# Differential-attention group of a two-layer encoder: another split of PSUM's eight banks, and most scores issued a step earlier

## The reference

```python
logits = jnp.einsum('bqhid,bshid->bhiqs', qb, k).astype(f32) * scale
bias = -slopes[:, None, None, None] * jnp.abs(qp[:, None] - pos[None, :])[None, None]
p = jax.nn.softmax(logits + bias, axis=-1)
a = (p[:, :, 0] - lam * p[:, :, 1]).astype(v.dtype)
return jnp.einsum('bhqs,bshe->bqhe', a, v)
```

## Time and profile before

| | |
|---|---|
| Runs of the kernel before | 2979.78, 2980.28, 2980.36 us; median 2980.28 |
| Profiled execution | 2979.33 us, of which the span of its instructions is 2977.5 us |
| Group C, first layer | unit 8's first transposes start at 358.83 us, unit 15's at 481.40 us |
| Granted TensorE clock, mean | 0.996 |

### The profile page before, as it was taken

How to read it: one execution, slowest core, us unless ns; L and a number is a source line. 1 busy time by engine, 2 the same in 40 slices (tenths; PEclk the granted TensorE clock), 3 DMA queues, 4 the chain that set the end, 5 groups by cost and what they waited for, 6 DMA issues and landing times.

```text
span 2977.5 us, 36876 instructions
## 1 busy us (share of the span) xinstructions
PE 2894.3 (97%) x13564; PEld 2312.8 (78%) x13564; DVE 1996.1 (67%) x2316; ACT 1320.5 (44%) x1843; POOL 461.6 (16%) x243
## 2 busy tenths in 40 slices
PE   7999889999999999999999998899999999999998
PEld 6777656888888888888877785578888888888887
DVE  3987887992465555556678788889716565565555
ACT  4326888993322212222333287889824222212223
POOL 1211332233300000000131123322342000000002
PEclk9999999999999999999999999999999999999999
DMA  5455332432122111111135643234312111112102
GB/s 196 152 170 127 84 81 63 92 82 88 43 64 64 43 42 56 42 42 42 40 133 197 169 97 71 64 86 92 112 44 71 43 55 45 42 42 57 55 29 57
DMA packets 236372, 236.48 MB, mean 79 GB/s; under 512 B 59488, under 2 KB 199520, under 8 KB 236256
## 3 DMA queue, kind: packets, MB, share of 16 engines
q1 hardware_dynamic: 236256, 234.94, 27.9%
HBM read 184.04 MB, written 50.86 MB: 79 GB/s over the span
## 4 chain that ended last, share of the span: by engine, by line
PE 87%; DVE 6%; issue 4%; ACT 2%; DMA 1%; SPq 0%; POOL 0%; ACTq 0%; DVEq 0%
PE ps L1815 31%; PE ps L1830 16%; PE ps L1554 16%; PE ps L1654 8%; PE ps L1726 6%; PE ps L1692 3%; PE ps L1693 3%; DVE ps L1255 2%; PE ps L1688 2%; PE ps L1795 1%; PE ps L1585 1%; PE ps L1739 1%; DVE prob L1327 1%; DVE r L1240 0%; DVE rinv L1322 0%
## 5 line engine op out<-in xcount | busy, mean ns | idle before, releaser
L1654 PE MATMUL ps<-stack 128*128 128x512 f32 (+1 forms) x1152 | 346.0, 418 | 44.1 <-ACT prob L928 19.1
L1453 DVE TENSOR_TENSOR xT<-ps,xT 128x512 f32<-128x512 f32 x352 | 241.5, 691 | 210.1 <-PE ps L1830 209.8
L1654 PEld LDWEIGHTS ps<-stack 128*128 128x128 f32 (+1 forms) x1152 | 205.9, 190 | 154.6 <-ACT prob L928 51.2
L1726 PEld LDWEIGHTS ps<-cst,prob 128*128 128x128 f32 x2048 | 254.7, 142 | 89.6 <-issue 19.8
L1726 PE MATMUL ps<-cst,prob 128*128 128x128 f32 x2048 | 310.7, 275 | 7.8 <-issue 4.1
L928 ACT ACTIVATE prob<-ps,nmx 128x1024 f32<-128x1024 f32 x256 | 284.7, 1112 | 22.7 <-PE ps L1726 12.3
L1363 DVE TENSOR_TENSOR ptl<-ps,pth 128x512 fp32r<-128x512 f32 x384 | 259.4, 685 | 48.8 <-ACT pth L990 42.2
L1418 DVE SCALAR_TENSOR_TENSOR cv<-u,vec,cv 128x1024 f32<-128x1024 f32 x176 | 225.8, 1283 | 89.0 <-ACT cv L1069 78.7
L1081 ACT ACTIVATE ah<-cv 128x1024 fp32r<-128x1024 f32 x44 | 46.7, 1061 | 528.9 <-DVE cv L1431 528.9
L1815 PE MATMUL ps<-xgh,w0h 128*128 128x512 f32 x704 | 274.7, 390 | 0.0
L1815 PE MATMUL ps<-xgl,w0h 128*128 128x512 f32 x704 | 273.9, 389 | 0.0
(11 more groups left out here) (247 smaller groups left out, 5565.4 us busy)
## 6 DMA issues: line engine op xcount, KB each, us to landing
wraw<-in_w_up SPq DMA_DIRECT2D x88, 512.0 KB, 4.9
draw<-in_w_down SPq DMA_DIRECT2D x22, 1024.0 KB, 4.9
stack<-ka_d SPq DMA_DIRECT2D x64, 256.0 KB, 5.8
wraw<-in_w_in SPq DMA_DIRECT2D x30, 512.0 KB, 4.1
vst<-v_d SPq DMA_DIRECT2D x48, 256.0 KB, 3.8
x_d<-xT SPq DMA_DIRECT2D x2, 4096.0 KB, 17.9
wraw<-in_w_out SPq DMA_DIRECT2D x16, 512.0 KB, 5.5
stack<-qc_d SPq DMA_DIRECT2D x64, 128.0 KB, 3.4
```

The source lines that it names most:

```text
L1453: ins = dve.tensor_tensor(xs, ps[:, 4 + j % 4, :], xs, ALU.add)
L1654: ins = pe.matmul(score_banks(i)[:, kh, :], st[q][0:rows, c0:c0 + P], st[k][0:rows, kh * HALF:(kh + 1) * HALF], start=n == 0, stop=n == le ...
L1726: ins = pe.transpose(ps[:, 4 + s % 2, m * P:(m + 1) * P], prob[:, b, m, s * P:(s + 1) * P], ident)
```

## The change

- For C from its third unit on (unit 10), scores go to three pairs of banks (0-1, 2-3, 4-5) by the table `PAIRS`. Units 8 and 9 keep two pairs.
- All of C has one transposing bank (6) and one value bank (7). The factor goes to bank 2 (bank 5 in units 8 and 15).
- TensorE, for items of units from 10 on: item 0 in step 5, item 1 in 6, item 2 in 7, items 3, 4, 5 in steps 0, 1, 2; items 6 and 7 stay in steps 4 and 5, and step 3 has no score. Items 1 (from unit 11) and 2 to 5 wait for the exponential three items back; items 0, 6 and 7 still wait for that of two items back. For unit 10, items 0 and 1 are both in step 6 (the latter waits for two items back).
- Each step's transposes wait for ScalarE's copy of the step before (`pt_hi`).
- Value product 0 of a unit (step 3) waits until the unit before has been read out of the value bank (`o_ready`, in unit 8 `o_read`).
- The factor's transposes move from step 6 to step 3, after that value product; they wait for the exponential of item 3. ScalarE's copy of the factor moves from step 7 to step 4.
- VectorE's `sum_output` in step 3 moves from behind item 5's maximum to ahead of it. In unit 8 ScalarE's `copy_part` moves ahead of the exponential of step 3.

VectorE's order of maxima and mixes and ScalarE's order of exponentials are otherwise as they were.

```diff
-        def score_banks(i):
-
-            return ps[:, 2 * ((i + 1) % 2):2 * ((i + 1) % 2) + 2, :]
+        PAIRS = (1, 2, 0, 1, 2, 0, 2, 0)
+        NORM_PAIR = 1
+        def score_pair(x, i):
+            c = x["k"] - U_C
+            if x["group"] != "C" or c < 2:
+                return (i + 1) % 2
+            return PAIRS[i]
+        def score_banks(x, i):
+            n = 2 * score_pair(x, i)
+            return ps[:, n:n + 2, :]
+        def trans_bank(x, s):
+            return ps[:, 6 if x["group"] == "C" else 4 + s % 2, :]
+        def value_bank(x):
+            return 7 if x["group"] == "C" else 6 + x["half"]
+        def norm_bank(x):
+            if x["group"] != "C":
+                return 7 - x["half"]
+            return 5 if x["k"] in (U_C, U_A - 1) else 2 * NORM_PAIR
+        def score_steps(x):
+            if x["group"] != "C":
+                return STEP_OF[own_items(x)]
+            return STEP_OF[6] if x["k"] < U_C + 2 else {0: 3, 1: 4, 2: 5, 4: 6, 5: 7}
+        def early_score_steps(x):
+            if x["group"] != "C" or x["k"] < U_C + 2:
+                return {s: (i,) for s, i in EARLY_STEP_OF[x["group"]].items()}
+            return {6: (0, 1), 7: (2,)} if x["k"] == U_C + 2 else {5: (0,), 6: (1,), 7: (2,)}
...
                 def act_unit(x, prev, nx, after):
                     for s in range(8):
                         second = nx and nx["group"] == "C"
+                        if s == 3 and x["k"] == U_C:
+                            copy_part(prev)
...
-                        if s == (7 if x["group"] == "C" else 6):
+                        if s == (4 if x["group"] == "C" else 6):
                             copy_norm(x)
...
+                        if s == 3 and x["group"] == "C":
+                            sum_output(prev)
                         if nx and s in STEP_OF[own_items(nx)]:
                             max_item(nx, STEP_OF[own_items(nx)][s])
...
-                    pe.wait_ge(exp_done, l * NS + it - 1 + EXP_CREDIT)
+                    c = x["k"] - U_C if x["group"] == "C" else 0
+                    far = (c >= 2 and 2 <= i <= 5) or (c > 2 and i == 1)
+                    pe.wait_ge(exp_done, l * NS + it - (2 if far else 1) + EXP_CREDIT)
+                    if (i == 0 and (c > 2 or x["k"] == U_A)) or (i == 1 and c == 2):
+                        pe.wait_ge(norm_copied, l * NU + x["u"] - 2 + 1 + N_CREDIT)
...
                 def transposed_free(x, prev, s):
 
+                    if x["group"] == "C":
+                        if s == 0:
+                            pe.wait_ge(norm_copied, l * NU + x["u"] + N_CREDIT)
+                        pe.wait_ge(pt_hi, l * (8 * NU) + x["u"] * 8 + s)
+                        return
+                    if x["k"] == U_A and s == 1:
+                        pe.wait_ge(norm_copied, l * NU + x["u"] + N_CREDIT)
                     y, n = (x, s - 1) if s >= 2 else (prev, s + 7)
...
+                        if s == 0 and x["k"] == U_C:
+                            pe.wait_ge(o_read, l * NAB + x["u"] + O_CREDIT)
+                        elif s == 0:
+                            pe.wait_ge(o_ready, l * NU + x["u"] + O_CREDIT)
                         pe.wait_ge(pt_hi, l * (8 * NU) + x["u"] * 8 + s + 1)
-                        pe.matmul(ps[:, 6 + b, :], vfull[x["par"]][:, s, :], ptf[:, s % NPT, :],
+                        pe.matmul(ps[:, value_bank(x), :], vfull[x["par"]][:, s, :], ptf[:, s % NPT, :],
                                   start=s == 0, stop=s == 7).then_inc(av_done, 1)
                         return
...
                 def pe_unit(x, prev, nx, after):
                     b = x["half"]
                     for s in range(8):
-                        if nx and s in STEP_OF[own_items(nx)]:
-                            score_item(nx, STEP_OF[own_items(nx)][s])
-                        if after and s in EARLY_STEP_OF[after["group"]]:
-                            score_item(after, EARLY_STEP_OF[after["group"]][s])
+                        if nx and s in score_steps(nx):
+                            score_item(nx, score_steps(nx)[s])
+                        for i in early_score_steps(after).get(s, ()) if after else ():
+                            score_item(after, i)
                         if s == 0:
                             if x["group"] == "C":
                                 pe.wait_ge(mixed_first, l * (2 * NC * NPM) + NPM * (x["u"] - U_C + 1))
@@ -1723,20 +1777,25 @@
 
                         transposed_free(x, prev, s)
                         for m in range(4):
-                            ins = pe.transpose(ps[:, 4 + s % 2, m * P:(m + 1) * P], prob[:, b, m, s * P:(s + 1) * P], ident)
+                            ins = pe.transpose(trans_bank(x, s)[:, m * P:(m + 1) * P], prob[:, b, m, s * P:(s + 1) * P], ident)
                         ins.then_inc(trans_done, 1)
                         if s >= LAG:
                             value_product(x, s - LAG)
                         elif prev:
                             value_product(prev, 8 + s - LAG)
-                        if s == 6:
+                        if s == (3 if x["group"] == "C" else 6):
                             pe.wait_ge(dinv_done, l * NU + x["u"] + 1)
-                            if prev and prev["group"] == "C":
+                            if x["group"] == "C":
+                                if x["k"] == U_C:
+                                    pe.wait_ge(pt_lo, l * (8 * NAB) + U_C * 8 + PT_CREDIT)
+                                elif nx["group"] == "C":
+                                    pe.wait_ge(exp_done, l * NS + nx["item0"] + 4 + EXP_CREDIT)
+                            elif prev and prev["group"] == "C":
                                 pe.wait_ge(o_ready, l * NU + prev["u"] + 1 + O_CREDIT)
                             elif prev:
                                 pe.wait_ge(o_read, l * NAB + prev["ab"] + 1 + O_CREDIT)
                             for m in range(4):
-                                ins = pe.transpose(ps[:, 7 - b, m * P:(m + 1) * P], dinv[:, m:m + 1].to_broadcast([P, P]), ident)
+                                ins = pe.transpose(ps[:, norm_bank(x), m * P:(m + 1) * P], dinv[:, m:m + 1].to_broadcast([P, P]), ident)
                             ins.then_inc(norm_done, 1)
                         if x["k"] == NU - 1 and s in (2, 3):
                             sum_squares_c(s - 2)
```

## The result

The changed kernel takes 2986.34 us, the median of 9 runs (2985.61 to 2991.00), against 2980.28, the median of 9 runs of the kernel before (2977.10 to 2983.43, so an unchanged kernel spreads over 6 us and not only over the 0.6 of the three runs given above). The ratio of the two is 1.0025 with a 95% interval of 1.0017 to 1.0033: the change makes the kernel slower, by 5 to 10 us. Its profiled execution took 2985.61 us with a span of 2983.8 at a mean granted clock of 0.997.

The account below looks back on a forecast made before the run. In C a chain passing between engines was taken as the bound. Per layer 0.44 + 3.98 + 0.87 + 0.1 = 5.4 us, two layers 10.8: profiled 2979.33 becomes 2990.1, median 0.95 above, so 2991; range 2982 to 3003.

Parts of the forecast that it names:

- the likeliest case: Whole kernel: slower, with C units of 17.9 to 18.5 us and a time of 2987 to 2996; chance 0.63.
- the value wait: C, step 3: product 0 waits for `sum_output`, that for product 7; score 6 stands behind; unit 18.20 us, before 17.54.
- Rival A: C units: three score pairs win and the value bank's wait hides; VectorE bounds at 15.8 us, time 2961; chance 0.11.
- Rival B: C units: gains and losses cancel; value bank's wait costs 0.6 us less, 17.6 a unit, time 2982; chance 0.11.
- the edges: C's first and last units: +0.44 us in unit 8, 0.67 in unit 9's steps, +0.87 behind unit 14, 0.1 in unit 15.
- the sum on record: C unit from item 0's maximum over product 7, `sum_output`, product 0, factor, score 6 and maximum 6: 18.20 us.
- The transposing bank: C steps: one bank's 1.45 us between transposes hides in a 1.76 step with score; 0.1 in all in unit 15.
- transposes that wait for copies: C, TensorE in the changed profile: such waits (L990) would show that the margins there were too fine.
- The early scores: C, maxima 3 and 5: idle 1.03 and 0.47 us shrink; taken alone, 1.7 us a unit won.
- The next unit: Unit 9's steps: score 1 of unit 10 waits for exponential 7, exponential 1 comes 0.67 us late; unit takes 18.87.
- The tail: End of C, item 0 of unit 15 to that unit's first transposes: 21.84 us, before 20.97, so +0.87.
- rival C: C units: TensorE's idle time lowers the clock, or copies' thin margin becomes a wait; 1 us a unit, 3003; chance 0.15.

Follow-up runs that it names:

- the first experiment: The kernel before with one edit: group C transposes into one bank, each step waiting for the copy of the step before; 2981.48 us, ratio 0.9998.
- the kernel with two pairs: Changed kernel with product 0 in step 4, `sum_output` behind maximum 5, factor's copy in step 3, but two score pairs and old score steps; 2986.76 us, ratio 1.0021.

## Why the prediction was right, and where its sizes were off

The range (2982 to 3003) holds the time, and the likeliest case, slower by the value wait, is what happened. Rival A needed product 7 to come 1.3 us sooner than 9.95 behind item 0's maximum; it comes at 402.10 - 392.17 = 9.93. Rival B asked that the value wait cost 0.6 less a unit than worked out; it costs 0.06 to 0.23 less.

The time alone would not have settled this. The forecast was 2991, with 2987 to 2996 as its own range, and the median of 2986.34 lies just under that; it is inside the stated range only because the range reached down into B. B's own figure is also wrong: units of 17.6 and the edges as worked out (0.44, 0.67, 0.87, 0.1) add 2.39 us a layer and give 2985, not 2982, so the median lies nearer to B than to the forecast. What speaks for the forecast are the units, 17.97 to 18.14 long and not 17.6, and the 9 us between the traces. Of the 10.8 us forecast, 8.9 are in the traces; the medians' 6.1 is smaller because of the clock, as the section on the hardware works out.

**The chain of a unit.** The unit from 392.17 to 410.30, link by link, beside the sum on record:

| link | predicted | measured |
|---|---|---|
| item 0's maximum to `sum_output` | 11.16 | 10.99 |
| `sum_output` to product 0 | 0.80 | 0.94 |
| product 0 to the factor | 0.86 | 0.94 |
| factor to score 6 | 0.36 | 0.35 |
| score 6 to maximum 6 | 0.92 | 0.91 |
| maximum 6 to the next item 0 | 4.10 | 4.00 |
| unit | 18.20 | 18.13 |

The mis-sized links nearly cancel here. Product 7's hand-over to VectorE was taken at 0.19 from a score's and is 0.04: 402.10 + 1.02 to 403.16. The waits stacked at product 0 add 0.15 in every second unit, which the shown one is; product 0 to the factor takes 0.08 more, and the way from maximum 6 to the next item 0 takes 0.10 less. That this unit's sum is right to 0.07 is thus partly luck; the odd ones are 0.2 shorter than the sum. The four steady units come to 18.06 in the mean, so 0.57 less than forecast for the four.

**The transposing bank** was costed at nothing beside steps with a score: the first experiment shows it. The prediction named transposes that wait for copies as a sign that its margins were too fine. Such waits are there, 35 in the first experiment and 13 in the changed kernel, of up to 1.0 us, but they delay nothing that counts. In a unit of the changed kernel a weight load waits 0.19 in step 1 and 0.69 in step 3, where TensorE then waits for `sum_output` anyway, and the transposes of steps 1 and 2 come 7.74 and 9.50 behind item 0's maximum, where 7.76 and 9.52 were worked out. **The early scores** were costed at nothing as long as the value wait stands behind them: shown by the kernel without them (90.54 against 90.63). VectorE was predicted to be ready for `sum_output` at 9.9 and is, at 401.88 + 0.14 - 392.17 = 9.85.

**The edges.** Unit 8 was put at +0.44 and costs +0.70. Two errors and a gain that was not foreseen make this up. Maximum 6 comes 0.79 later than before (368.16 and 369.28, less the 0.33), not 0.44. A mix behind it then takes 1.28 in place of 1.78; before, GpSimd's multiplication (L697, 369.33 to 370.60) ran beside it, now it ends as the mix starts. No run shows whether that is the reason. So maximum 7 is only 0.21 late (371.60 and 372.14, less the 0.33):

```profile
369.90 1.78 DVE L1327 SCALAR_TENSOR_TENSOR prob<-prob1a,rinv,prob 128x1024 f32<-128x1024 f32 x1
```

```profile
370.94 1.28 DVE L1364 SCALAR_TENSOR_TENSOR prob<-prob1a,rinv,prob 128x1024 f32<-128x1024 f32 x1
```

The first row is the kernel before. The other 0.49 comes from a step that was missed, which ScalarE and GpSimd of the changed kernel show:

```profile
369.67 1.28 POOL L732 TENSOR_TENSOR osum<-osum,nrm 64x512 f32<-64x512 f32 x1
...
371.04 0.60 ACT L999 ACTIVATE nrm<-ps 128x512 f32<-128x512 f32 x1 [0.88 <-POOL osum L732]
371.53 1.11 ACT L963 ACTIVATE prob<-ps,nmx 128x1024 f32<-128x1024 f32 x1
...
372.62 0.60 ACT L1027 ACTIVATE ptf<-ps 128x512 f32<-128x512 f32 x1
373.46 1.11 ACT L963 ACTIVATE prob1b<-ps,nmx 128x1024 f32<-128x1024 f32 x1 [0.24 <-DVE nmx L1292]
```

The factor's copy, moved three steps up, is not free in unit 8: it overwrites `nrm`, which GpSimd still reads for the last unit of B, in a multiplication that stands behind its mix of tile 0. ScalarE stands still 0.88, the exponential behind it is late, and with it score 0 of unit 10, for which VectorE waits 0.34 at 373.77. That the earlier factor copy costs nothing was checked against who asks for the copy, not against who still reads its target. The next unit was put at 18.87 and takes 18.40: exponential 1 is held up by 0.46 (380.11, that is 1.78 behind maximum 1 at 378.33 in place of 1.32) and not by 0.67, and the links behind it are those of an odd unit, 0.2 shorter than the sum. The tail was +0.87 and is +0.75; unit 15's steps +0.1 and +0.08. Together 5.4 us a layer were predicted and 4.47 are there: the steady units 0.57 less, unit 10's edge 0.47 less, the tail 0.12 less, unit 8's edge 0.26 more.

**The clock (rival C).** The trace of the changed kernel keeps 1.00 through C; no unit loses 1 us. In unit 8's steps TensorE stands idle for 0.73 and 1.14 us with one score between, a little less than the 2 us foreseen, and in this execution nothing comes of it.

## What to carry to other kernels

Giving up a bank's second copy costs what waiting for its read-out adds to the chain that bounds the stage. Before a bank is given away, follow the instruction that would wait for the read-out, and everything queued behind it on its engine: for transposes nothing was queued that mattered, for values the score on which the next maximum hangs. When a fix for one wait brings nothing, look for a second wait that ends at the same time before calling the fix useless: here the early scores were worth nothing with it and an estimated 6 us without it. Moving one value product into the next step and one multiplication behind the next maximum, with the factor's copy, one score and a redundant wait moved along, turned 0.25% lost into 0.19% won. A copy that moves earlier must be checked against the last reader of its target, on every engine: this was missed twice, in unit 8 of the change (0.88 us) and in the kernel with two pairs (0.67 to 0.86 us in every unit). And two kernels that differ in one thing do not price that thing if something else was tuned for only one of them.

## What the runs showed of the hardware

**The low clock comes and goes between executions.** The kernel before, group A in the first layer, and the changed kernel over the same stretch, both with TensorE busy (columns as in the earlier trace rows):

```profile
674.00:677.00 3.00, 3.00 (x14) 2.70 (x14) 0.92 (x2) 0.60 (x1) 1.27 (x1) 0.51 0.58 235
677.00:680.00 3.00, 3.00 (x12) 2.42 (x11) 1.08 (x3) 2.27 (x4) 0.00 (x0) 0.50 0.01 3
```

```profile
674.00:677.00 3.00, 3.00 (x27) 2.91 (x27) 1.38 (x2) 2.04 (x4) 0.14 (x1) 1.00 1.03 396
677.00:680.00 3.00, 3.00 (x27) 2.88 (x26) 1.38 (x2) 1.26 (x3) 0.53 (x1) 1.00 1.02 414
```

By this the distance between the two executions, 4.8 us at unit 30's factor, falls to 2.2 at unit 31's (680.02 and 682.26). Ahead of this drop TensorE was hardly idle: it was busy for 2.63, 2.80 and 3.00 of the three stretches of 3 us before 674. In the kernel without the `norm_copied` wait it happened in unit 9's steps:

```profile
375.00:378.00 3.00, 1.14 (x4) 0.58 (x4) 2.92 (x8) 1.86 (x5) 0.00 (x0) 1.00 0.88 228
378.00:381.00 3.00, 3.00 (x9) 1.76 (x8) 2.93 (x5) 0.60 (x1) 0.00 (x0) 0.50 1.03 217
```

1.14 of 3 us busy, then 0.50 with TensorE busy throughout, and the unit takes 20.52 in place of 18.40. The changed kernel is busy for 1.13 of 3 us at the same point of the work (372 to 375) and the clock stays at 1.00. So this drop has idle time ahead of it, as rival C had it, but like idle time does not always bring one, and the first drop came without much of it. The Trainium skill (TensorE: Matmul & The Clock Gate) has idleness put the clock to its lower level; the level agrees with the rows (0.50, 1.2 GHz), the cause only with the second drop, and what decides between two executions is shown by no run here. The times go with the mean granted clock of their runs. Of the 55 runs of the kernel before made beside the experiments, the 7 at 0.997 took 2976.26 to 2978.89 us (median 2977.39) and the 15 at 0.994 took 2980.58 to 2983.08 (median 2982.16): 4.8 us for 0.003, about two such drops. Five of the changed kernel's 9 runs were at 0.997 and took 2985.61 to 2986.34 (median 2985.89). At the same granted clock the two kernels are thus 8.5 us apart, close to the traces' 9; the medians are only 6.1 apart because the changed kernel's runs had more of the full clock. Whether the change has a part in that or it is chance is shown by no run: in the kernel without the early scores, whose units are as long, 2 of 10 runs were at 0.997.

**A multiplication on the upper half of the partitions starts later.** In the kernel before, `sum_output` of the unit with the other head starts 0.17 us late (420.44 behind a maximum that ends its slot at 420.27; the one at 402.88 follows at once). Its own slot is 0.73 in place of 0.61, and that of the maximum behind it 1.25 in place of 1.15. The view doesn't name partitions; `sum_output` of such a unit works on partitions 64 to 127, by `rows` in L1340. Together 0.39 us: this is the 17.77 of the earlier trace rows against the 17.38 of the unit before it. The Trainium skill (VectorE: DVE Perf Modes, Two Vector instructions with no wait between them) has a model in which an instruction whose partitions start in another quadrant than those of the last is held until all before it have finished; these rows agree, with 0.39 us in a unit. In the changed kernel `sum_output` waits for product 7 anyway, and the difference is no longer visible in the length of a unit.
